# Causal differential attention in a two-layer hybrid kernel: transposes behind the cross products, VectorE's steps reordered, v rounded tile by tile

## The reference

```python
h = h + 0.5 * swiglu(rms_norm(h, ffn1_norm), ffn1_wgu, ffn1_wd)      # hidden 2816
q, k, v, gu, gv = split(rms_norm(h, mix_norm) @ w_in)                # 5 x 512 columns
q, k = partial_rope(q), partial_rope(k)                              # 4 heads x 2 branches x 64
for each block of 128 queries:                                       # causal
    p1 = softmax(where(causal, q[..., 0, :] @ k[..., 0, :].T / 8, -1e30))
    p2 = softmax(where(causal, q[..., 1, :] @ k[..., 1, :].T / 8, -1e30))
    attn = (p1 - lam * p2) @ v                                       # per head, v is 128 wide
attn = rms_norm(attn, subln) * (1 - lam_init)
gm = chunked_spatial_gating(gelu(gu), gelu(gv), ...)
h = h + concat(attn, gm) @ w_out
kv = rms_norm(mem, mem_norm) @ cross_wkv                             # 256 x 2048
h = h + cross_attention(rms_norm(h, cross_norm), kv, cross_wq, cross_wo)
h = h + 0.5 * swiglu(rms_norm(h, ffn2_norm), ffn2_wgu, ffn2_wd)
```

## Time and profile before

| | before |
|---|---|
| median of 3 runs | 2118.1 us |
| the profiled execution's own time | 2117.83 us |
| its span in the profile | 2115.9 us |
| PE matmul, busy | 2086.1 us, 99% |
| PE weight load, busy | 1865.3 us, 88% |
| VectorE (DVE), busy | 1646.2 us, 78% |
| ScalarE (ACT), busy | 980.7 us, 46% |
| granted TensorE clock, mean | 0.996 |
| chain that ended last | PE 92%, DVE 5%, ACT 2% |

### The profile page before, as it was taken

One profiled execution on the slowest core, in us unless ns is written; L12 is line 12 of the kernel. 1 busy time (PEld: TensorE's weight loads), 2 busy tenths in 40 slices (PEclk: granted clock), 3 DMA queues, 4 the chain that ended last, 5 costly groups with the idle time before them and its releaser, 6 DMA issues.

```text
span 2115.9 us, 32572 instructions
## 1 busy us (share of the span) xinstructions
PE 2086.1 (99%) x13115; PEld 1865.3 (88%) x13115; DVE 1646.2 (78%) x2466; ACT 980.7 (46%) x1481; POOL 150.5 (7%) x114
## 2 busy tenths in 40 slices
PE   8999999999999999999999999999999999999998
PEld 6899998888888889999889999988898888999997
DVE  7998887657655789888799988766686458898885
ACT  6444444345444545444454444444454345444442
POOL 0000003100020300000020000030001102000001
PEclk9999999999999999999999999999999999999999
DMA  6332322422221243332233333242232214333321
GB/s 195 100 110 90 110 85 97 138 80 80 100 100 60 85 130 110 97 118 90 70 120 110 110 106 109 65 142 98 79 102 100 80 61 130 100 110 96 105 85 55
DMA packets 267952, 212.12 MB, mean 100 GB/s; under 512 B 7358, under 2 KB 234268, under 8 KB 267804
## 3 DMA queue, kind: packets, MB, share of 16 engines
q1 hardware_dynamic: 264544, 205.55, 31.1%
q10 hardware_dynamic: 3260, 4.51, 0.8%
HBM read 207.93 MB, written 2.10 MB: 99 GB/s over the span
## 4 chain that ended last, share of the span: by engine, by line
PE 92%; DVE 5%; ACT 2%; issue 1%; DMA 0%; POOL 0%; POOLq 0%; DVEq 0%; ACTq 0%
PE ps L1920 19%; PE ps L1921 19%; PE ps L1922 19%; PE ps L2116 11%; PE ps L2118 11%; PE ps L2117 11%; DVE w_lo L1178 1%; DVE ex L1786 1%; DVE mx L1766 1%; ACT w_hi L664 1%; ACT ex L1057 1%; PE ps L2263 0%; PE ps L2448 0%; PE ps L1958 0%; PE ps L2341 0%
## 5 line engine op out<-in xcount | busy, mean ns | idle before, releaser
L1921 PE MATMUL ps<-hid_lo,wn_hi 128*128 128x512 f32 x640 | 251.7, 393 | 0.0
L1920 PE MATMUL ps<-hid_hi,wn_hi 128*128 128x512 f32 x640 | 251.6, 393 | 0.0
L1922 PE MATMUL ps<-hid_hi,wn_lo 128*128 128x512 f32 x640 | 249.0, 389 | 0.0
L1434 DVE SCALAR_TENSOR_TENSOR h<-ps,h 128x512 f32<-128x512 f32 x224 | 152.4, 683 | 31.3 <-PE ps L1922 31.0
L664 ACT ACTIVATE w_hi<-raw 128x2048 fp32r<-128x2048 f32 x61 | 116.7, 1913 | 124.7 <-PE ps L1922 92.6
L2116 PE MATMUL ps<-t_hi,form_hi 128*128 128x256 f32 x576 | 159.7, 277 | 0.9 <-DVE G L1346 0.9
L2118 PE MATMUL ps<-t_hi,form_lo 128*128 128x256 f32 x576 | 159.6, 277 | 0.0
L2116 PE MATMUL ps<-hn_hi,form_hi 128*128 128x256 f32 x576 | 159.5, 277 | 0.0
L2118 PE MATMUL ps<-hn_hi,form_lo 128*128 128x256 f32 x576 | 159.4, 277 | 0.0
L2118 PE MATMUL ps<-t_hi,more_lo 128*128 128x256 f32 x576 | 159.3, 277 | 0.0
L2117 PE MATMUL ps<-t_lo,form_hi 128*128 128x256 f32 x576 | 159.2, 276 | 0.0
(11 more groups left out here) (334 smaller groups left out, 5959.4 us busy)
## 6 DMA issues: line engine op xcount, KB each, us to landing
sraw<-in_ffn_wgu_dram SPq DMA_DIRECT2D x144, 512.0 KB, 4.8
raw<-in_ffn_wd_dram SPq DMA_DIRECT2D x48, 512.0 KB, 3.8
raw<-in_ffn_wd_dram SPq DMA_DIRECT2D x80, 256.0 KB, 4.1
raw<-in_w_in_dram SPq DMA_DIRECT2D x40, 512.0 KB, 4.4
raw<-in_cross_wkv_dram SPq DMA_DIRECT2D x32, 512.0 KB, 4.0
raw<-in_ffn_wgu_dram SPq DMA_DIRECT2D x30, 512.0 KB, 4.8
raw<-in_w_out_dram SPq DMA_DIRECT2D x16, 512.0 KB, 3.9
raw<-in_cross_wq_dram SPq DMA_DIRECT2D x16, 512.0 KB, 4.0
```

Source lines behind the costliest of these rows:

```text
L1434: dve.scalar_tensor_tensor(out=h[:, m, :], in0=ps[:, down_bank(c, m), :], scalar=0.5, in1=h[:, m, :], op0=ALU.mult, op1=ALU.add).then_inc( ...
L1920: pe.matmul(dst, a_hi, b_hi, start=start, stop=False)
L1921: pe.matmul(dst, a_hi, b_lo, start=False, stop=False)
L1922: return pe.matmul(dst, a_lo, b_hi, start=False, stop=stop)
```

## The change

- **v by tiles.** In the second unit of v, PE counts `v_done` up at the end of each of the first three tiles, and ACT's `v_hi` of a tile waits for its own tile. Ahead of them ACT runs an exponential of one column, into a place that is overwritten later.
- **PE's step.** `cross_kv` comes right after the scores, then `head_values` where there is one, and the transposes last, in all steps. In step 16 the transposes stand between the `w_out` products of k = 4, 5 and those of k = 6, 7.
- **Banks.** The second cross unit (n = 1, steps 2 and 3) goes into bank 1 instead of 2. It waits for the `v_lo` of the second tile, unit 2 waits for unit 0's `kv_ready`, and the values of head 0, also in bank 1, for unit 1's.
- **DVE's step.** The order is now: `maxima`; `turned_low` of the transposes of step s-1 (not in the late steps; for steps 4, 8, 12 and 16 at the step's own end instead); half of a split, first half in even and second in odd steps; in odd steps `kv_low`; `attn_weights`.
- **ACT's step.** `exponentials`, `kv_high` in odd steps, `turned_high`, `round_unit` in odd steps. The rounding keeps its place at the end of odd steps.

```diff
@@ ACT @@
-                act.wait_ge(w_used, used(L, VV + 1))
+                act.activation(sm[:, 0, 0:1], ident[:, 0:1], ACT.Exp)
                 for t in range(ST):
+                    if t < ST - 1:
+                        act.wait_ge(v_done, L * 3 + t + 1)
+                    else:
+                        act.wait_ge(w_used, used(L, VV + 1))
                     act.activation(v_hi[:, t, :], ps[:, t, :], ACT.Copy, scale=rtok[:, t:t + 1])\
...
+                def kv_bank(n):
+                    return 1 if n == 1 else 2
...
                 for s in range(22):
-                    late = s % 4 == 1 and s > 1
-                    if 1 <= s < 17 and not late:
-                        turned_high(s)
                     if s < 16:
                         exponentials(s)
...
                     if s % 2 and s < 16:
                         kv_high(s)
-                    if s < 17 and late:
+                    if 1 <= s < 17:
                         turned_high(s)
@@ DVE @@
                     if s < 16:
                         maxima(s)
                     if s == 0:
                         gate_chunk(3)
-                    if s % 2 and s <= 17:
-                        split_half(L, CK + s // 2 + 1, 1)
-                    if 1 <= s < 17 and not late:
-                        turned_low(s)
+                    if 2 <= s < 17 and s % 4 != 1:
+                        turned_low(s - 1)
+                    if 1 <= s <= 17:
+                        split_half(L, CK + s // 2 + 1, s % 2)
+                    if s % 2 and s < 16:
+                        kv_low(s)
                     if s < 16:
                         attn_weights(s)
                     if s == 0:
                         low_gm(3)
-                    if s % 2 and s < 16:
-                        kv_low(s)
-                    if s < 17 and late:
-                        turned_low(s)
-                    if s % 2 == 0 and s <= 16:
-                        split_half(L, CK + s // 2 + 1, 0)
+                        split_half(L, CK + 1, 0)
...
+                    if s in (4, 8, 12, 16):
+                        turned_low(s)
@@ PE @@
                     if hd:
                         pe.wait_ge(attn_final, L * 4 + hd)
+                    else:
+                        pe.wait_ge(kv_ready, L * 8 + 2)
...
                     if c == 0:
                         wait_unit(L, CK + n)
-                        if n:
-                            pe.wait_ge(kv_ready, L * 8 + n)
+                        if n >= 2:
+                            pe.wait_ge(kv_ready, L * 8 + (1 if n == 2 else n))
                         else:
-                            pe.wait_ge(v_ready, L * 4 + 3)
+                            pe.wait_ge(v_ready, L * 4 + kv_bank(n) + 1)
...
-                    if 1 <= s < 17 and not late:
-                        turn_weights(s)
                     if s < 16:
                         cross_kv(s)
                     if late:
                         head_values((s - 5) // 4)
-                    if s < 17 and late:
+                    if s == 16:
+                        wait_unit(L, WO)
+                        attn_out(0, [4, 5])
+                    if 1 <= s < 17:
                         turn_weights(s)
                     if s == 16:
-                        wait_unit(L, WO)
-                        attn_out(0, [4, 5, 6, 7])
+                        attn_out(0, [6, 7])
```

More of the change, by code:

```diff
@@ L300, in macaron_kernel @@
         sq_ready = sem("sq_ready")
+        v_done = sem("v_done")
         sum_ready = sem("sum_ready")
@@ L1065, in kv_high @@
                     act.activation(kc_hi[:, 2 * n:2 * n + 2, :] if n < 4 else vc_hi[n - 4][:, :, :],
-                                   ps[:, 2, :].rearrange("p (k c) -> p k c", c=M), ACT.Copy)\
+                                   ps[:, kv_bank(n), :].rearrange("p (k c) -> p k c", c=M), ACT.Copy)\
                        .then_inc(kv_rounded, 1)
                 for s in range(22):
-                    late = s % 4 == 1 and s > 1
-                    if 1 <= s < 17 and not late:
-                        turned_high(s)
                     if s < 16:
@@ L1794, in kv_low @@
                               else (vc_hi[n - 4][:, :, :], vc_lo[n - 4][:, :, :]))
-                    dve.tensor_tensor(out=lo, in0=ps[:, 2, :].rearrange("p (k c) -> p k c", c=M),
+                    dve.tensor_tensor(out=lo, in0=ps[:, kv_bank(n), :].rearrange("p (k c) -> p k c", c=M),
                                       in1=hi.bitcast(f32), op=ALU.subtract).then_inc(kv_ready, 1)
@@ L2197, in head_norm, with token_unit @@
                     broadcast(rh, 3, orb_done)
-            def token_unit(L, u, s, bank, n_tok, src_hi, src_lo, stage=None, wait=None):
+            def token_unit(L, u, s, bank, n_tok, src_hi, src_lo, stage=None, wait=None, tile_done=None):
                 wait_unit(L, u)
@@ L2211, in token_unit @@
                                        src_lo[:, k, t * P:(t + 1) * P], w1, w2, k == 0, k == KT - 1)
+                        if tile_done is not None and k == KT - 1 and t < n_tok - 1:
+                            last.then_inc(tile_done, 1)
                 return last.then_inc(w_used, 1)
@@ L2307, in _ @@
                     token_unit(L, VV + s, s, 0, ST, hn_hi, hn_lo,
-                               wait=lambda t: pe.wait_ge(qkT_ready, L * 8 + 4 + t + 1))
+                               wait=lambda t: pe.wait_ge(qkT_ready, L * 8 + 4 + t + 1), tile_done=v_done)
                     mix_chunk(2 + s)
@@ L2348, in cross_kv @@
                         wait_unit(L, CK + n)
[L2349 to L2350 removed]
+                        if n >= 2:
+                            pe.wait_ge(kv_ready, L * 8 + (1 if n == 2 else n))
                         else:
[L2352 removed]
+                            pe.wait_ge(v_ready, L * 4 + kv_bank(n) + 1)
                     for k in range(KT):
[L2354 removed]
+                        dst = ps[:, kv_bank(n), c * M:(c + 1) * M]
                         if n < 4:
```

## The result

The changed kernel takes 2106.8 us (median of 5 runs, 2105.9 to 2107.2) against 2118.1 (5 runs, 2117.6 to 2118.2): the ratio is 0.9946, interval 0.9933 to 0.9959, or 11.3 us less. The forecast was 2105.4 in a range of 2103.8 to 2110.5.

A forecast was written before the change was run, and what follows sets the result against it. PE, busy in 99% of the span, was taken as the bound, with only its holes to win: -13.5 us plus 2 x (0.2+0.1+0.1) of new holes gives -12.7, forecast 2105.4 us, range 2103.8 to 2110.5.

The forecast's parts named there:

- new holes: Waits that the new order opens in each layer's attention stage: 0.2 us at step 4, 0.1 each at 8 and 12.
- rival 2: PE's matmul row, not load starts, gives what can be won: 10.0 us, so 2108.9; chance 0.08.
- (a): v rounded tile by tile with an early exponential: closes a 1.02 us hole before the first cross product.
- (b): PE's cross products ahead of the transposes: 2.8 us of cover for the wait for ex, crossings costing nothing.
- crossings: PE's passages into and out of the 64-row scores: 0 change, bounds -1.6 to +3 us in all.
- (c): DVE's kv_low ahead of attn_weights: closes kv_ready holes, 0.27 us at steps 4, 8, 12 and 0.49 at 2.
- The 0.2 at step 4: Transposes of step 4 would wait 0.2 us for step 3's wT_lo, a 4.26 us chain against PE's 4.09.
- (d): Step 16, w_out products of two k ahead of the last transposes: closes a hole of 1.2 us.
- rival 1: Partial gain: wider waits at steps 4, 8, 12 and crossings at their upper bound, -8.2 us, 2110; chance 0.20.
- Rival 3: No change: DVE's in-order queue paces the stage, waits return at other steps, under 4 us won; chance 0.07.
- Rival 4: Slower: kv_low blocks DVE at odd steps; at 1.2 us of PE wait each, +3.3 us, 2121.4; chance 0.05.
- likeliest case: The forecast 2105.4 with its own range 2103.8 to 2106.8: no new hole and crossings at lower bound, or twice the new holes.

The follow-up runs named there:

- seven pairs: Changed kernel with the scores of steps 1 and 2, 3 and 4, up to 13 and 14 done back to back on PE: 2108.7 us, ratio 0.9955.
- three pairs: Changed kernel with only the scores of steps 5 and 6, 9 and 10, 13 and 14 done back to back: 2104.9 us, ratio 0.9938.
- half of the reordering: Two runs on the changed kernel: PE's transposes back between scores and products, 2168.2 us; or DVE's and ACT's orders as before, 2144.2 us.
- tail alone: Kernel before the change with only step 16's order changed, last transposes between the w_out products: 2117.4 us, ratio 0.9997.

## Why the prediction was right, and by how much it was off

**What could be won.** Counted by load starts it was 13.5 us, by PE's matmul row 10.0. The stages got 12.0 us shorter, with 0.3 of new holes (4 x 0.08) and 1.2 of dearer groups in them: 12.0+0.3+1.2=13.5 were closed. Smaller terms nearly cancel in this sum: passages 0.1 us a layer dearer, the products' own loads 0.2 closer together. More was won than the 10.0 us of the matmul row, so load starts were the right measure, and rival 2 falls. The Trainium skill (Perfetto Trace Analysis, Identifying the Most-Contended Engine) says that weight loads tell more than matmul busy time. The trace after the change agrees with it as the one before did: 12.0 us won against 10.0 in the matmul row.

**(a) v by tiles**: right. Undone it costs 2.1 us in the stages, for a forecast of 2 x 1.02, and the early exponential was rightly priced at nothing.

**(b) PE's order.** The cover held: no wait for `ex` is left. The crossings are **the term of the sum that was mis-sized**. I took 0 in bounds of -1.6 to +3; they cost +1.2 us. The passages out of the scores (0.26) and from products to transposes (0.13) came out as I read them. The one from transposes to scores was read at a single transpose: 0.26 holds at three places a layer, and it is 0.30 to 0.31 at the six others. What was missed altogether is that transposes behind products are 0.04 us a group dearer than behind masks, and 0.17 at step 16.

The runs with paired scores tell more of it. There some groups wait, and load behind the same products with an idle in between; they are short again, 0.42 for four (step 4 of seven pairs, then step 16 of three pairs):

```profile
500.72 0.42 PEld L2351 LDWEIGHTS ps<-ident,ex 128*128 128x128 f32 x4 [0.63 <-issue]
```

```profile
554.97 0.19 PEld L1928 LDWEIGHTS ps<-gm_hi,w_lo 128*128 128x128 f32 x1
555.37 0.42 PEld L2351 LDWEIGHTS ps<-ident,ex 128*128 128x128 f32 x4 [0.21 <-issue]
```

So it is not the shape of what precedes them, but that they follow products at once. At step 16 they gain nothing by it: from the last product's load to the end of the group it is 555.37+0.42-554.97=0.82 us with the idle, and 556.88+0.59-556.65=0.82 in the changed kernel without it. That the loads queue behind products still running would fit; no run shows it by itself.

**(c) DVE's order.** The new holes at steps 8 and 12 were forecast at 0.1 and measured at 0.08. The 0.2 at step 4 did not come. My chain was 4.26 us from the last product's load; it took 499.05-495.19=3.86, most of the difference being its first term, 0.43 in place of 0.71, since the exponentials didn't keep ACT from `kc_hi`. PE was there after 4.19, at its usual 0.13 behind the products, with 0.3 us to spare. The timeline of step 4:

```profile
495.19 0.19 PEld L1928 LDWEIGHTS ps<-mg_hi,w_lo 128*128 128x128 f32 x1
...
495.62 0.60 ACT L1073 ACTIVATE kc_hi<-ps 128x512 fp32r<-128x512 f32 x1
...
498.50 0.55 DVE L1781 TENSOR_TENSOR wT_lo<-ps,wT_hi 128x384 fp32r<-128x384 f32 x1
...
499.38 0.46 PEld L2351 LDWEIGHTS ps<-ident,ex 128*128 128x128 f32 x4
```

The bank of its own does what was argued: without it 2.1 us more in the stages, in steps 2 and 4.

**(d) Step 16**: right in the changed kernel, but for a reason that I had counted only in part. Its cover alone brought 0.3 to 0.4 us a layer in the profile and nothing that the runs can tell (ratio 0.9997); it needs `turned_low(16)` behind the evacuation in DVE's queue, which (c) brings.

**Rivals.** Of rival 1 about a quarter is true, the crossings (1.2 of its 4.5 us); its wider hand-overs did not come, as 0.08 at steps 8 and 12 shows. Rival 3 falls with the stage lengths. Rival 4's mechanism exists: with only half of the reordering, waits on DVE's queue return at each step, and the kernel is 26 or 50 us slower than before. My working of DVE's order from step 0 to 10 excluded it for the change as a whole, and rightly so.

**The sum.** -12.7 was forecast. With the new holes at 0.3 instead of 0.8 it is -13.2, and with 1.2 for the dearer groups -12.0, as measured in the stages. The two misses are of opposite sign, so the forecast looks closer than its terms were. The likeliest case's own range doesn't follow from the ends that it names, either: no new hole and crossings at -1.6 give 2103.0, twice the new holes 2106.2, where it says 2103.8 and 2106.8. The measured 2106.8 lies 0.6 us beyond that case as it should have been bounded, and inside the whole range. The remaining 0.7 us between 12.0 and the 11.3 of the medians lies outside: the start of the first stage differs by up to 1.3 us (478.8 to 480.1) among kernels that are alike up to there.

## What to carry to other kernels

Where one engine is busy in 99% of the span, count its holes by the starts of its weight loads, and for each wait write down which instruction it waits for and what stands ahead of that one in its own engine's queue: the large misses here (tail alone, half reorderings, paired scores) were all such a place in a queue. A reordering over three in-order engines is one change; its halves cost 26 and 50 us where the whole won 11. Once the holes are closed, the passages between shapes are the next thing, and they pay only at steps where the producers have slack.

## What was not expected of the hardware

Holes can cost more than their length. Behind a hole of 2.54 us that ended a stretch of full work, the granted clock went from 1.00 to 0.50 (2.4 to 1.2 GHz) for some 3 us, and 1.6 us were lost on top; with many holes of 2 to 3 us a quarter of the excess was the clock (7 to 8 of some 31 us a layer). It doesn't come each time: the same hole in layer 1 cost 2.5 us. Nor does it need so long a hole: in the kernel with only step 16 changed, layer 0 had it behind the first cross product's 1.1 us (windows as above):

```profile
482.00:486.00 4.00, 4.00 (x24) 3.87 (x24) 2.79 (x9) 3.10 (x7) 0.00 (x0) 0.58 0.00 0
```

The hole ended at 481.17, with 1.09 us of idle. The same hole in the kernel before left the clock at 1.00, and so it did in layer 1 of this kernel and in both layers where v waits for the whole unit. What decides it no run shows.
